# Twenty places for expert weights instead of eighteen, and final additions made in PSUM, in a mixture-of-experts layer

## The reference, cut to what matters

```python
h  = rms_norm(x, norm1_g) * (1 + sc1) + sh1
proj = h @ w_in
a  = pool_mix(proj[..., :512]);  b = conv_mix(proj[..., 512:])
m  = sigmoid(h @ gate_w + gate_b), split in two, times a and b, added
x  = x + g1 * (m @ w_out)
h2 = rms_norm(x, norm2_g) * (1 + sc2) + sh2
# top 4 of 32 experts per row, softmax weights in combine[:, e]
for e in range(32):
    gt = minimum(h2 @ exp_w_gate[e] + exp_b_gate[e], 7)
    up = clip(h2 @ exp_w_up[e] + exp_b_up[e], -7, 7)
    act = gt * sigmoid(1.702 * gt) * (up + 1)
    out += combine[:, e:e+1] * (act @ exp_w_down[e] + exp_b_down[e])
x = x + g2 * out
y = rms_norm(x, final_g)
```

## Time and profile before

| what | value |
|---|---|
| time, median of three runs | 1152.16 us (1151.28 to 1153.07) |
| span of the profiled execution (first to last instruction) | 1150.3 us |
| PE busy | 1122.8 us, 98% of the span |
| DVE, ACT, POOL busy | 497.9, 181.4, 29.8 us |
| HBM read | 454.40 MB |
| DMA, whole span | 397 GB/s |
| granted TensorE clock | 0.998 of full speed |

### The profile page before, as it was taken

How to read it: one execution, slowest core, us unless ns; L and a number is a source line. 1 busy time by engine, 2 the same in 40 slices (tenths; PEclk the granted TensorE clock), 3 DMA queues, 4 the chain that set the end, 5 groups by cost and what they waited for, 6 DMA issues and landing times.

```text
span 1150.3 us, 16135 instructions
## 1 busy us (share of the span) xinstructions
PE 1122.8 (98%) x5962; PEld 457.5 (40%) x5963; DVE 497.9 (43%) x1134; ACT 181.4 (16%) x343; POOL 29.8 (3%) x78
## 2 busy tenths in 40 slices
PE   8999999999999999999999999999999999999996
PEld 6676675633333333333333333333333333333332
DVE  3498425653344433444333433343334433333334
ACT  4101301311111111111111111111111111111112
POOL 4002300000000000000000000000000000000000
PEclk9999999999999999999999999999999999999999
DMA  9988688699999999999999999999999999999995
GB/s 342 374 288 297 245 305 303 229 419 417 427 428 428 428 428 428 428 428 428 428 428 428 428 428 428 428 428 428 428 428 428 428 428 428 428 428 429 426 422 228
DMA packets 59022, 456.15 MB, mean 397 GB/s; under 512 B 7237, under 2 KB 26497, under 8 KB 31349
## 3 DMA queue, kind: packets, MB, share of 16 engines
q1 hardware_dynamic: 54880, 452.35, 94.9%
q10 hardware_dynamic: 4117, 3.47, 1.2%
HBM read 454.40 MB, written 1.40 MB: 396 GB/s over the span
## 4 chain that ended last, share of the span: by engine, by line
PE 77%; DMA 21%; DVE 1%; issue 0%; SPq 0%; ACT 0%; DVEq 0%
PE bank L1731 46%; DMA arena<-in_exp_w_up 10%; DMA arena<-in_exp_w_gate 10%; PE bank L1509 6%; PE bank L1456 4%; PE bank L1758 4%; PE bank L1675 4%; PE bank L1596 2%; PE bank L1813 1%; PE bank L1579 1%; PE bank L1683 1%; PE bank L1430 1%; PE bank L1749 1%; PE bank L1687 1%; PE bank L1378 1%; PE bank L1689 0%
## 5 line engine op out<-in xcount | busy, mean ns | idle before, releaser
L1731 PE MATMUL bank<-ring,arena 128*64 128x512 f32 x2112 | 469.9, 595 | 10.2 <-DMA ring<-in_exp_w_gate 9.7
L1731 PEld LDWEIGHTS bank<-ring,arena 128*64 128x64 f32 x2112 | 146.3, 137 | 310.0 <-issue 283.7
L1731 PE MATMUL bank<-arena 128*64 128x512 f32 x1056 | 235.9, 595 | 4.2 <-DMA arena<-in_exp_w_gate 4.0
L1731 PEld LDWEIGHTS bank<-arena 128*64 128x64 f32 x1056 | 73.6, 137 | 153.8 <-issue 138.5
L821 ACT ACTIVATE arena<-arena 32x256 f32<-32x256 f32 x136 | 56.0, 412 | 421.1 <-DVE arena L1200 419.9
L1291 DVE TENSOR_SCALAR arena<-bank 128x512 f32<-128x512 f32 x33 | 22.8, 691 | 166.6 <-PE bank L1731 166.6
L1284 DVE TENSOR_SCALAR arena<-bank 128x512 f32<-128x512 f32 x33 | 22.8, 691 | 166.5 <-PE bank L1731 166.5
L1306 DVE TENSOR_TENSOR arena<-bank,biases 128x512 f32<-128x512 f32 x66 | 42.5, 686 | 109.9 <-PE bank L1731 109.9
L1269 DVE TENSOR_TENSOR x<-x,bank 128x512 f32<-128x512 f32 x132 | 84.5, 681 | 12.6 <-PE bank L1758 12.6
L834 ACT ACTIVATE arena<-arena 128x512 f32<-128x512 f32 x33 | 20.8, 629 | 353.8 <-DVE arena L1284 353.8
L1758 PE MATMUL bank<-arena 64*128 64x512 f32 x264 | 65.6, 615 | 0.0
(11 more groups left out here) (312 smaller groups left out, 739.8 us busy)
## 6 DMA issues: line engine op xcount, KB each, us to landing
ring<-in_exp_w_gate SPq DMA_DIRECT2D x42, 2048.0 KB, 27.8
ring<-in_exp_w_up SPq DMA_DIRECT2D x41, 2048.0 KB, 28.2
ring<-in_exp_w_down SPq DMA_DIRECT2D x40, 2048.0 KB, 29.1
arena<-in_exp_w_gate SPq DMA_DIRECT2D x21, 2048.0 KB, 25.7
arena<-in_exp_w_up SPq DMA_DIRECT2D x20, 2048.0 KB, 27.3
arena<-in_exp_w_down SPq DMA_DIRECT2D x20, 2048.0 KB, 30.0
ring<-in_w_ada SPq DMA_DIRECT2D x24, 1024.0 KB, 10.7
ring<-in_gate_w SPq DMA_DIRECT2D x8, 1024.0 KB, 8.6
```

The source lines that it names most:

```text
L1731: ins = mm(out[64 * hh:64 * hh + 64, :], lhs(k), w[:, D * (k % 2) + HALF * hh:D * (k % 2) + HALF * (hh + 1)], start=(done is y_mm and k == ...
```

## The change

The places grow to 20 (10 pairs). The tokens x, the normed rows and many other buffers, which were tiles of their own or lay elsewhere in `arena`, get new addresses in a bigger `arena`; some buffers now share one place (`gmin` with `xg`, `actT` with `acts`). The four arena pairs are EARLY_PAIR, SAMPLE_PAIR (where the sample's modulation rows lay), MERGED_PAIR (where the mixers' result lay) and NORM_PAIR (with the prompt's modulation rows in its second half). The turn grows to five experts (10 pairs come round after five), 32 being six turns and two. The waits ahead of the loop, the first refills and the very last load (now in two rows, the second with a semaphore of its own) follow. At the end TensorE first writes x into the banks by products with the identity, and scatters on top; ACT squares and DVE's last step read PSUM, and the sample's stores go to ACT's queue.

```diff
-EARLY_PAIR, LATE_PAIR, LAST_PAIR = ARENA - 4096, 7168, 3072
+MERGED_PAIR = WEIGHTED_AT + 288
+NORM_PAIR = MERGED_PAIR + 4096
+EARLY_PAIR = NORM_PAIR + 4096
+SAMPLE_PAIR = 2 * D
-PAIRS = 9
-TURN = 3
-SPLIT, HALVED, LAST_HALVES = 4, 3, (1, 2, 3, 5)
+PAIRS = 10
+TURN = 5
+SPLIT, HALVED, LAST_HALVES = 4, 2, (1, 2, 3, 5)
+NORM_SPLIT = 9
...
+                if i == order[4]:
+
+                    sp.wait_ge(cm_mm, KD)
+                    load_half(1, NORM_SPLIT, 0)
+                    sp.wait_ge(h2_ready, 1)
+                    sp.wait_ge(xs_ready, 1)
+                    load(1, PER_EXPERT + 1)
                 if i == SPLIT:
                     for half in range(2):
-                        sp.wait_ge(piece_used, front_use(i) - 1 + half)
+                        if half:
+                            sp.wait_ge(wo_mm, 6)
+                        else:
+                            sp.wait_ge(piece_used, front_use(i) - 1)
...
-            sp.wait_ge(logit_mm, TT)
-            load(1, PER_EXPERT + 1)
+            sp.wait_ge(ssq2, 6)
+            load(1, PER_EXPERT + 2)
             sp.wait_ge(h2_ready, TT + 1)
-            load(1, PER_EXPERT + 2)
+            load_half(1, NORM_SPLIT, 1)
...
+                    if half and rows_apart:
+                        for r, landed in enumerate((pair_ld[p], last_ld)):
+                            at_row = SLOT * half + D * r
+                            sp.dma_start(slots(2 * p + half, 1)[:, D * r:D * (r + 1)], w[:, i % 2, at_row:at_row + D]).then_inc(landed, 16)
+                        continue
...
+            act.wait_ge(logit_mm, 1)
+            for q in range(4):
+                ins = a.activation(quadrant(xs, q), quarter(x[0:NS_TOK, 2, :], q), ACT.Copy)
+            ins.then_inc(xs_ready, 1)
             act.wait_ge(x2_ready, 4)
...
-            act.wait_ge(h2_ready, TT + 1)
-            for q in range(4):
-                ins = a.activation(quadrant(xs, q), quarter(x[0:NS_TOK, 2, :], q), ACT.Copy)
-            ins.then_inc(xs_ready, 1)
...
+            def last_squares(t, hh):
+                act.wait_ge(last_mm, 3 * t + hh + 1)
+                a.activation(ring[:, JUNK + t, HALF * hh:HALF * (hh + 1)], last_bank(t, hh),
+                             ACT.Square, accum_out=stat[:, 18 + 3 * hh + t:19 + 3 * hh + t]).then_inc(ssq3, 1)
...
+            act.wait_ge(y_ready, 3)
+            for q in range(4):
+                act.dma_start(quarter(y_sample[0], q), y_s[32 * q:32 * q + 32, :]).then_inc(stored, 16)
...
-            v.memset(h2[:, 2, :], 0.0).then_inc(h2_zero, 1)
...
-            step(v.memset(oh, 0.0))
             step(v.memset(rt[:, 6, 2, :], 1.0))
...
             choose(2, 1)
+            step(v.memset(oh, 0.0))
...
+            dve.wait_ge(ssq3, 1)
+            last_mean(0, stat[:, 18:19])
+            dve.wait_ge(fg_ld, 16 * 5)
+            last_gain(0, 1)
+            finish(0, h2[0][:, halves[0]], last_bank(0, 0), fgb[:, halves[0]])
             dve.wait_ge(parts_mm, 1)
             last_mean(2, bank[2][:, 0:1])
+            dve.wait_ge(ssq3, 3)
+            last_mean(1, stat[:, 19:20])
+            finish(0, h2[0][:, halves[1]], last_bank(0, 1), fgb[:, halves[1]])
+            last_gain(2, 2)
+            finish(2, y_s, last_sample, fgq)
+            last_gain(1, 3)
+            for hh, cs in enumerate(halves):
+                finish(1, h2[1][:, cs], last_bank(1, hh), fgb[:, cs])
...
+            def carry(out, src):
+                mm(out, ident[:, :], src, start=True, stop=False, skip_group_check=True)
+
+            def last_scatter(t, hh):
+                mm(last_bank(t, hh), ohwT[64 * hh:64 * hh + 64, P * t:P * (t + 1)], ysb[64 * hh:64 * hh + 64, 0, :],
+                   start=False, stop=True, skip_group_check=True).then_inc(last_mm, 1)
+
+            for hh in range(2):
+                carry(last_bank(0, hh), x[:, 0, HALF * hh:HALF * (hh + 1)])
+            carry(last_sample, xs)
+            pe.wait_ge(y_ev, items * 2 + 1)
+            for hh in range(2):
+                last_scatter(0, hh)
+            carry(last_bank(1, 0), x[:, 1, 0:HALF])
+            pe.wait_ge(last_y, 1)
+            scatter_sample(last_sample, start=False).then_inc(last_mm, 1)
+            last_scatter(1, 0)
+            carry(last_bank(1, 1), x[:, 1, HALF:D])
+            last_scatter(1, 1)
             pe.wait_ge(same_made, 1)
             pe.wait_ge(parts_ready, 1)
             mm(bank[2][:, 0:4], same_row, part_sum[:, :], start=True, stop=True).then_inc(parts_mm, 1)
```

More of the change, by code:

```diff
@@ L144, in view @@
             return a
[L147 to L177, removed]
+        def front(start, *shape):
+            return view(FRONT_AT + start, *shape)
+        x = view(TOKENS_AT, TT, D)
+        xn = view(OLD_ROWS_AT, TT, D)
+        uc_ext = view(OLD_ROWS_AT, CT, CEXT)
+        yc = view(OLD_ROWS_AT + CT * CEXT, CT, CW)
+        hT = view(OLD_ROWS_AT + 2688, KD, TOK)
+        gates = front(2304, 2 * KD, TOK)
@@ new lines, in build @@
+        hS = front(2304, KD, TOK)
+        shT = front(8064, KD, 32)
+        group_of = front(8320, TOK)
+        pick = front(8608, 2, 2)
+        merged = front(6912, KD, TOK)
+        sig_g = front(6912, CT, TOK)
+        up_ext = front(9216, CT, PEXT)
+        pooled = front(10488, CT, TOK)
+        wsum = front(11640, 2, PEXT)
+        rows = front(12288, 3, HALF)
+        tmp = front(13824, CT, CW)
+        act_c = front(9216, CT, TOK)
+        slot_i = front(13824, SLOTS).bitcast(I32)
+        part_i = front(13824 + SLOTS, SLOTS).bitcast(I32)
@@ new lines, in build @@
+        n2rows = front(15120, HALF)[0:64, :]
+        bada = front(15632, HALF)[0:4, :]
+        ada_sel = front(16144, 4, 32)[0:4, :, :]
+        ada_bias = [front(16912, HALF), rows[:, 0, :]]
+        stage = front(16528, P)[0:N_COLS, :]
+        c_stage = front(16656, P)[0:2 * KD, :]
+        dwc = front(16784, CT, 32)
+        c_cols = front(17424, 2 * KD)
+        csig = front(17440, 2 * KD)
+        h2 = [view(NORMED_AT + D * t, D) for t in range(2)] + [biases[0:NS_TOK, 0, :]]
+        sh2b = [view(NORM_PAIR + SLOT + D, D), view(SAMPLE_PAIR + D, D)]
@@ L880, in _ @@
             v.tensor_copy(c_cols[:, :], bank[5][:, 0:2 * KD]).then_inc(c_cols_ready, 1)
-            squares = view(2304 + 2 * D, D)[0:NS_TOK, :]
+            squares = front(2304 + 2 * D, D)[0:NS_TOK, :]
             dve.wait_ge(x_ld[2], 16)
@@ L1073, in add_output @@
                     dve.wait_ge(x2_ready, after)
-                parts = [view(12288 + cs.start, cs.stop - cs.start)[0:r, :] for cs, _ in cuts]
+                parts = [parts_of[0:r, cs] for cs, _ in cuts]
                 for part, (cs, src) in zip(parts, cuts):
-                    v.tensor_tensor(part, src, g1b[0:r, t // 2, cs], ALU.mult).then_inc(wo_ev, 1)
+                    v.tensor_tensor(part, src, g1b[t // 2][0:r, cs], ALU.mult).then_inc(wo_ev, 1)
                 wo_reads[0] += len(cuts)
@@ L1337, in _, with finish @@
-            last_add(1, 0)
-            tile_mean(0)
-            last_add(1, 1)
+            def finish(t, out, src, gain):
+                v.scalar_tensor_tensor(out=out, in0=src, scalar=stat[:, 4 + t:5 + t], in1=gain,
+                                       op0=ALU.mult, op1=ALU.mult).then_inc(y_ready, 1)
+            halves = [slice(HALF * hh, HALF * (hh + 1)) for hh in range(2)]
+            dve.wait_ge(ssq3, 1)
+            last_mean(0, stat[:, 18:19])
+            dve.wait_ge(fg_ld, 16 * 5)
@@ L1728, in product @@
                         pe.wait_ge(pair_ld[q % PAIRS], g * (16 * TURN * PER_EXPERT // PAIRS) + 16 * (used + q // PAIRS + 1))
+                    elif last and done is y_mm and k == KD - 1:
+                        pe.wait_ge(last_ld, 16)
                     w = slots((PIECES * j + s) % (2 * PAIRS), 1)
```

199 lines of the change are left out of this document (84 added, 115 removed).

## The result

The changed kernel took 1186.12 us (1185.31 to 1187.19) against 1151.78 for the kernel before, measured beside it: a ratio of 1.0291 [1.0278, 1.0305]. It is slower by 3%, where 1148.4 was forecast. This is the third rival, the one with the smallest chance.

What follows compares the result with a forecast made beforehand. The prediction took the landing of the last expert weights, set by bytes landed before the stream became continuous, as the bound. Span 1150.3 - 4.8 (places) + 1.0 (end) = 1146.5; with 1.86 from span to median, 1148.4 us, range 1146.6 to 1151.2.

Steps and rivals of the forecast that it cites:

- rival 3: TensorE's expert loop: a five-expert body is not held, each of five jumps back waits for a fetch; 1175.6 us, chance 0.07.
- some six of them: TensorE's instruction store: five experts estimated at some six 16 KiB blocks of a 128 KiB store, so the body would fit.
- The point from which it decides: Jumps back in TensorE's loop: from 4.3 us a jump the fetch waits make the kernel slower than before.
- Part one, the places: Expert weight loads: a tenth pair of places lets the stream end one pair earlier; gain 4.8 us, ends 4.3 and 4.9.
- Pair 7: SyncE's loads ahead of the loop: issued at about 204.6 us, after the sample rows' norm and their copy.
- rival 1: Ahead of the loop: late broadcasts delay norm and loop start by 2.3 us, eating the gain; 1150.7 us, chance 0.18.
- the 2.45 that the prediction allowed: Broadcast rows for the sample norm: the new half load at 182.3 can delay them by its own transfer, 2.45 us.
- 6.6 us of cover: TensorE's turn at 207.67 us: its input was ready 6.6 us earlier, so a 2.45 us delay is covered.
- The load of 252.8: Weight load issued at about 252.8 us: still lands in about 8.5 us; if queued, the forecast is wrong.
- Things in front of the loop: New half load, moved copies and clears ahead of the loop: cost 0, with ends -0.4 and +2.3 us.
- Part two, the end: After the last product: identity products on TensorE and sample stores on ScalarE's queue cost +1.0 us, bounds -0.5 and +2.2.
- Rival 2: The end: identity products cost nothing because DVE was the busiest engine there; end at -0.5, 1146.9 us, chance 0.13.

Runs made afterwards that it cites:

- the two written-out forms: TensorE's loop over turns unrolled, in the changed kernel (1157.72 us, ratio to before 1.0037) and in the kernel before (1158.69 us, ratio 1.0048).
- nine pairs in the new layout: Changed kernel's addresses and waits with nine pairs, a turn of three, the old end and no tenth pair: 1153.99 us, ratio to before 1.0010.
- the resident pair: New layout, turn of three, old end; tenth pair outside the round, filled ahead of the loop for expert 30: 1149.28 us, ratio to before 0.9972.

## Why the prediction was wrong, point by point

**The loop body: the step that failed.** The prediction named the mechanism and its place (rival 3: each of five jumps back waits for a fetch) and gave it 0.07 "against: no stall shows today". The earlier trace rows show that three experts are held. They say nothing of five, and the rival was put down by a row of another size. What stood in place of a measurement was an estimate of the size and a capacity. The size was right: "some six of them" is 5.9 blocks by the counts above. The conclusion "so the body would fit" was wrong: four experts (4.7 blocks) are held, five (5.9) are not.

The Trainium skill (Runtime: NRT & Kernel Launch, Instruction fetch mechanics) gives TensorE a store of 128 KiB in blocks of 16, which is eight blocks; the runs show 5.9 blocks not held, so the size of the store alone does not decide. The same section's rule that a taken branch out of the window forces a fetch before execution goes on is what after does at each of its five jumps, with 7.1 to 8.2 us of wait; but the body of four experts jumps back six times without a fetch, so the window is wider than the two pages that the rule gives it.

**The rival's size.** It gave 1175.6, and 1186.1 was measured. It put 8.5 us on a jump, the price of an isolated 2 MB load; the wait was 7.1 to 8.2, a fair guess, but with the granted clock that fell in it the product that followed took 1.5 to 2.7 us longer than 7.02, and a jump 10.2 in all. That is 8.5 us more over five jumps. The loop started 1.55 later, and the end cost 1.5 more than thought. These 11.5 are the difference of the spans (1173.7 by the rival's terms, 1185.2). The point from which it decides, 4.3 us a jump, was far exceeded.

**Part one, the places: right.** 4.8 was forecast; 4.6 came out between the two written-out forms, with the change's half loads, waits and four arena pairs. SyncE's issues in after (start us, us with the waits between merged ones, line):

```profile
183.54 0.33 SPq L483 DMA_DIRECT2D ring<-in_exp_w_up  x1
183.91 0.43 SPq L489 DMA_DIRECT2D arena<-in_exp_w_up  x1
207.60 0.33 SPq L483 DMA_DIRECT2D arena<-in_exp_w_gate  x1
210.31 0.33 SPq L483 DMA_DIRECT2D ring<-in_exp_w_up  x1
...
221.78 0.33 SPq L483 DMA_DIRECT2D arena<-in_exp_w_up  x1
226.28 0.33 SPq L489 DMA_DIRECT2D arena<-in_exp_w_up  x1
```

The order is the one derived from the trace of before. Everything is 1.58 us later than in the earlier trace rows (183.54 against 181.96); with that taken off, the last three stand at 208.7, 220.2 and 224.7, where 208.73, 220.3 and 224.7 were derived. Pair 7 is the exception: 206.0 for 204.6, so the hole was 5 us long instead of gone. It came from the broadcasts, as rival 1 feared: the sample's norm stood 4.67 us for them instead of 3.32, and started 1.3 later than derived.

```profile
200.13 1.27 DVE L1119 SCALAR_TENSOR_TENSOR biases<-arena,stat 32x1024 f32<-32x1024 f32 x1 [4.67 <-DMA arena<-mod_rows]
```

Without the half pair, with nine pairs in the new layout, the same wait is 2.53; with the resident pair's half it is 7.17, and the norm 3.9 later than derived, more than the 2.45 that the prediction allowed. It did no harm in any of them: the turn on TensorE had 6.6 us of cover, and pair 3 waits for 208.7 anyway. The load of 252.8, issued at 254.20, landed in 9.9 us where 8.5 was foreseen (10.3 and 8.6 in the written-out forms): it was queued by some 1.4 us, which the prediction had called a sign of being wrong. The gain of a pair was there all the same.

**Things in front of the loop: right, though the line drawn was crossed.** "The forecast is wrong if the loop starts later than 229" was said, and it started at 230.43. But the whole delay was there at pair 2: from its issue to loop start it is 46.89 us in after and 46.92 in before (228.88 - 181.96), and the same to 0.2 us in all seven other traces. So the half pair, the moved copies and clears cost nothing, as forecast, and rival 1 (the gain eaten there) fell, though its delay of the broadcasts was real. What varies comes in ahead of 182 us, and it varies in kernels whose front is that of before too: 228.88 for before, 229.01 written out, 230.07 with a turn of six; the five kernels with the new layout lie between 229.72 and 231.43. Whether the new addresses add to it there is not shown. The bound on the loop start was drawn from one execution and was narrower than this.

**Part two, the end: mechanism right, size wrong.** +1.0 was forecast with +2.2 as the upper end; it costs 2.4 by the traces, past the 2.2 that was named as a sign of being wrong. The end of after, instructions in time (start us, us, engine, line; waits in brackets):

```profile
1170.10 1.99 PE L1868 MATMUL bank<-arena,ident 128*128 128x512 f32 x4
...
1172.44 1.13 PE L1871 MATMUL bank<-arena 64*128 64x512 f32 x4
1173.50 1.13 PE L1868 MATMUL bank<-arena,ident 128*128 128x512 f32 x2
...
1174.56 0.64 PE L1777 MATMUL bank<-arena 64*32 64x256 f32 x8
...
1175.12 1.12 PE L1871 MATMUL bank<-arena 64*128 64x512 f32 x2
...
1176.17 1.12 PE L1868 MATMUL bank<-arena,ident 128*128 128x512 f32 x2
...
1177.23 1.12 PE L1871 MATMUL bank<-arena 64*128 64x512 f32 x2
1178.28 0.39 PE L1888 MATMUL bank<-cT,upto 128*128 128x4 f32 x2
...
1180.21 2.13 ACTq L896 DMA_DIRECT2D out<-arena  x4
1180.28 1.41 DVE L1355 SCALAR_TENSOR_TENSOR arena<-bank,stat,ring 128x512 f32<-128x512 f32 x2
1181.06 0.99 SPq L573 DMA_DIRECT2D out<-arena  x2
```

With T at 1170.15: first scatter at T+2.3 (2.2 forecast), since the first identities ran closely, four records in 1.99. Behind it each single step starts 1.05 to 1.06 after the one ahead, whether identity or scatter, where 0.89 less an overlap of 0.2 and 0.85 had been put down. Two halves side by side also take 1.06, so a split scatter costs as much as both halves together. TensorE is done at T+8.1, not 7.3. VectorE catches up a part: last row at T+11.5 (11.0 forecast), last store of SyncE issued at T+11.9 (11.45). ScalarE's four stores took 2.13 us against SyncE's 1.73, until T+12.2; from the last issue to the end of the span it is then 2.8 us, where it was 2.3 before. The forecast had hoped for 0.2 less there. Rival 2, identities for nothing, fell.

## What to carry to other kernels

Before a loop body is made longer, find out whether its instructions will be held: that no blocks of instructions come between two turns of the old body shows only that the old size fits, and a body of the new size can be measured alone, without the rest of the change, by one number. When extra space is won, it need not enter the rotation that sets the length of the body: a buffer beside it, for data that is used once behind the loop, gave most of the gain at the old length. And work taken over by an engine that stands last in the chain is priced by the start-to-start distance of single products there, not by the time per product in a long run.

## What the runs showed of the hardware that was not expected

- A body of 4.7 blocks of 16 KB (by the counts of fetched blocks) on TensorE is held over the jump back, one of 5.9 is not; a jump to code that is not held costs 7.1 to 8.2 us of standing, and about 10.2 in all with the product after it, which starts at the lower granted clock (0.51).
- Code written out in a straight line never made TensorE wait for a fetch visibly, yet the kernel before became 5.5 us slower by it: the stream of weights ended with about 5 us at half its rate. The blocks of instructions use the same DMA engines, 1.06 us each; that they fall on half of them is a reading of the sizes and stays open.
- On TensorE, single products of 512 columns in turn, identity or scatter, started 1.06 us apart, though in a run of eight each took 0.89.
